# Where the modulation of a second block is summed: from the expert stages to the projections and the gated layers, in 1024-column steps

## The reference

```python
mod = (jax.nn.silu(c) @ w_ada[l] + b_ada[l])[:, None, :]          # c: [1, 1024], w_ada: [1024, 9 * 1024]
sh1, sc1, gt1, sh2, sc2, gt2, sh3, sc3, gt3 = jnp.split(mod, 9, axis=-1)
n = modulate(rmsnorm(h, g_ffn1[l]), sh1, sc1)                     # n * (1 + scale) + shift
h = h + 0.5 * gt1 * swiglu(n, w1_gate[l], w1_up[l], w1_down[l])
n = modulate(rmsnorm(h, g_mix[l]), sh2, sc2)
h = h + gt2 * hybrid_mixer(n, w_in[l], w_pool[l], pool_scale[l], w_out[l])
n = modulate(rmsnorm(h, g_ffn2[l]), sh3, sc3)
h = h + 0.5 * gt3 * swiglu(n, w2_gate[l], w2_up[l], w2_down[l])
```

## Time and profile before

| what | value |
| --- | --- |
| median of 3 runs | 1484.13 us (1484.05 to 1486.57) |
| the profiled execution: its time, its span | 1485.72 us, 1483.6 us |
| PE busy | 1410.2 us, 95% |
| VectorE busy | 971.9 us, 66% |
| ScalarE busy | 697.3 us, 47% |
| moved by the DMA engines | 266.48 MB, mean 180 GB/s |

### The profile page before, as it was taken

One profiled execution on the slowest core, in us unless ns is written; L12 is line 12 of the kernel. 1 busy time (PEld: TensorE's weight loads), 2 busy tenths in 40 slices (PEclk: granted clock), 3 DMA queues, 4 the chain that ended last, 5 costly groups with the idle time before them and its releaser, 6 DMA issues.

```text
span 1483.6 us, 16900 instructions
## 1 busy us (share of the span) xinstructions
PE 1410.2 (95%) x6579; PEld 1149.5 (77%) x6579; DVE 971.9 (66%) x1449; ACT 697.3 (47%) x1014; POOL 18.6 (1%) x41
## 2 busy tenths in 40 slices
PE   7979999999999998999999999989999899899997
PEld 5856677888888877777887887778888787778885
DVE  4577647677577777667767678745777557544444
ACT  6464536434343567453343443644434455443442
POOL 0000000000000000000000000000000000000000
PEclk9987999999999998999999999999999999999999
DMA  8440015466555542044665666534656452455530
GB/s 330 171 146 1 1 64 220 158 266 256 234 227 230 227 168 89 29 152 179 266 247 230 267 255 266 194 119 174 251 227 232 189 196 86 131 188 181 195 114 29
DMA packets 37902, 266.48 MB, mean 180 GB/s; under 512 B 4525, under 2 KB 5040, under 8 KB 6080
## 3 DMA queue, kind: packets, MB, share of 16 engines
q1 hardware_dynamic: 36720, 262.65, 46.8%
q0 software_dynamic: 960, 2.52, 0.6%
q10 hardware_dynamic: 144, 0.24, 0.0%
HBM read 264.34 MB, written 1.05 MB: 179 GB/s over the span
## 4 chain that ended last, share of the span: by engine, by line
PE 88%; DVE 8%; ACT 2%; issue 1%; DMA 0%; POOL 0%; DVEq 0%; ACTq 0%; POOLq 0%
PE ps L373 25%; PE ps L375 24%; PE ps L374 24%; DVE wl L1138 2%; PE ps L391 2%; PE ps L552 2%; PE ps L489 1%; PE ps L649 1%; DVE AR L1301 1%; DVE KL L1206 1%; PE ps L467 1%; PE ps L477 1%; ACT XN L835 1%; PE ps L470 1%; PE ps L454 1%
## 5 line engine op out<-in xcount | busy, mean ns | idle before, releaser
L1138 DVE TENSOR_TENSOR wl<-ring,wh 128x2048 fp32r<-128x2048 f32 x208 | 471.7, 2288 | 162.6 <-ACT wh L823 162.3
L373 PE MATMUL ps<-wh,XH 128*128 128x512 f32 x1216 | 481.8, 396 | 6.6 <-DVE wl L1138 5.1
L375 PE MATMUL ps<-wh,XL 128*128 128x512 f32 x1216 | 475.4, 391 | 0.0
L374 PE MATMUL ps<-wl,XH 128*128 128x512 f32 x1216 | 474.8, 390 | 0.0
L823 ACT ACTIVATE wh<-ring 128x2048 fp32r<-128x2048 f32 x208 | 393.4, 1912 | 144.7 <-PE ps L375 144.2
L373 PEld LDWEIGHTS ps<-wh,XH 128*128 128x128 f32 x1216 | 229.3, 189 | 55.3 <-issue 6.0
L375 PEld LDWEIGHTS ps<-wh,XL 128*128 128x128 f32 x1216 | 229.1, 188 | 48.7
L374 PEld LDWEIGHTS ps<-wl,XH 128*128 128x128 f32 x1216 | 229.6, 189 | 46.0
L373 PE MATMUL ps<-wh,HT 128*128 128x512 f32 x448 | 176.9, 395 | 6.0 <-DVE HT L1393 4.5
L375 PE MATMUL ps<-wh,HT 128*128 128x512 f32 x448 | 174.6, 390 | 0.0
L374 PE MATMUL ps<-wl,HT 128*128 128x512 f32 x448 | 174.4, 389 | 0.0
(11 more groups left out here) (235 smaller groups left out, 1150.3 us busy)
## 6 DMA issues: line engine op xcount, KB each, us to landing
ring<-stream_dram SPq DMA_DIRECT2D x248, 1024.0 KB, 7.0
H<-x_dram SPq DMA_DIRECT2D x2, 512.0 KB, 4.7
out_dram<-XN SPq DMA_DIRECT2D x2, 512.0 KB, 2.7
XN<-ag_dram POOLq DMA_DIRECT2D x1, 768.0 KB, 4.6
AR<-pT_dram POOLq DMA_DIRECT2D x2, 256.0 KB, 3.0
AR<-g_final_dram POOLq DMA_DIRECT2D x1, 512.0 KB, 4.1
ring<-stream_dram SPq DMA_DIRECT2D x2, 144.0 KB, 5.4
VBK<-w_pool_dram POOLq DMA_DIRECT2D x1, 256.0 KB, 3.3
```

What stands on the lines that cost most here:

```text
L373: e.matmul(o, ah, bh, start=start, stop=False)
L374: e.matmul(o, ah, bl, start=False, stop=False)
L375: return e.matmul(o, al, bh, start=False, stop=stop)
L1138: e.tensor_tensor(wl[:, k % WBUF, :], ring[:, n % RING, :], h.bitcast(F32), ALU.subtract).then_inc(up("wlo", ("wlo", k)))
```

## The change

The nine parts are made elsewhere: part 0 in nsa (4 quarters in 4 steps, at `kv0`, `kv1`, `kv2`, `q0`), part 1 in moba (4 quarters in 3 steps, at `skv`, `bq0`, `bq1`: 1, 1, 2), parts 2 to 6 in `ffn1` (20 quarters in 10 pairs, two a pair), part 7 in the mixer (3 steps, 1, 1, 2), part 8 in `ffn2` (4 quarters in 6 pairs). The expert stages have none. A quarter is now two of the eight rows of each partition over all 1024 columns of the part: one chunk, two instructions of 1024 columns. The biases of shifts and scales come as 48 columns of the constants and are added after the turn (one more tensor_tensor, 128 x 8); the bias row is left for the gates. `silu(c)` is made in nsa. Sums: part 0 after `q1`, part 1 after `bq1`, part 7 after `z3`, part 8 in `ffn2`; in `ffn1` parts 2 to 5 at pairs 2, 4, 6, 8 and part 6 at 11, that is behind the last `down`.

```diff
-ADA = {0: (0, 1, 3), 1: (2, 5, 4, 6), 2: (7, 8)}
+ADA = {"nsa": (0,), "moba": (1,), "ffn1": (2, 3, 4, 5, 6), "mixer": (7,), "ffn2": (8,)}
+ADA_STEPS = {"nsa": 4, "moba": 3, "ffn1": 10, "mixer": 3, "ffn2": 6}
...
-        return [("ada", v[:, :, 256 * q:256 * q + 256]) for q in ada_quarters(l, j)]
+        return [("ada", v[:, 2 * (q % 4):2 * (q % 4) + 2, 1024 * (q // 4):1024 * (q // 4) + 1024]) for q in ada_quarters(stage, j)]
...
-    for c in (1024, 1536, 2048):
-        plan += w_cols(w_in, c, 512)
-    plan += compress("a_ck_w1") + w_cols(w_in, 0, 512) + compress("a_cv_w1") + w_cols(w_in, 512, 512)
+    for i, c in enumerate((1024, 1536, 2048)):
+        plan += w_cols(w_in, c, 512) + ada("nsa", i)
+    plan += compress("a_ck_w1") + w_cols(w_in, 0, 512) + ada("nsa", 3) + compress("a_cv_w1") + w_cols(w_in, 512, 512)
...
+            plan += w_cols(w["w_kv_shared"], 0, 512) + ada("moba", 0)
+            for i, c in enumerate((0, 512)):
+                plan += w_cols(w["b_w_q"][0], c, 512) + ada("moba", i + 1)
...
-        plan += pairs_plan(16, gu, down, lambda j: ada(l, j))
+        plan += pairs_plan(16, gu, down, lambda j: [])
...
+        for stage in ("ffn1", "ffn2"):
+            for j in range(12):
+                ada_due[stage, j] = [q // 4 for i in ((j - 1,) if j < 10 else () if j == 10 else (9, 10)) for q in ada_quarters(stage, i) if q % 4 == 3]
...
                 project("bq1", "mix1", lambda t: [("bqsq", 1, t)])
+                ada_sum(1)
                 turn_heads(("bt", 0), QN[:, :, 0:512], 8, [("bn", 0)])
...
+                    take(len(ada_quarters("nsa", c)))
...
+            def ada_turned(part):
+                c = 2 * (part // 3) + part % 3
+                dst = MT[:, 8 * c:8 * c + 8]
+                for hf in range(2):
+                    e.wait_ge(*at("adasum", part, hf))
+                    e.tensor_reduce(dst[:, 4 * hf:4 * hf + 4], ps("ada", part, hf)[:, :].rearrange("p (a n) -> p a n", a=4), AX,
+                                    ALU.add).then_inc(up("dve", ("turnsum", part, hf)))
+                e.wait_ge(*at("turnsum", part, 1))
+                e.tensor_tensor(dst, dst, col("ab", 8 * c, 8), ALU.add).then_inc(up("dve", ("mod", part)))
...
+            def ada_take(q):
+                take()
+                part, f, a = q // 4, q % 4, ACC[q // 4]
...
+                for t in range(2):
+                    c, v = SC8[:, 2 * f + t:2 * f + t + 1], r[:, 1024 * t:1024 * t + 1024]
+                    if f + t == 0:
+                        ins = e.tensor_scalar(a, v, c, None, ALU.mult)
+                    else:
+                        e.wait_ge(*at("adaq", 8 * part + 2 * f + t - 1))
+                        ins = e.scalar_tensor_tensor(out=a, in0=v, scalar=c, in1=a, op0=ALU.mult, op1=ALU.add)
...
                     e.tensor_reduce(ss2[:, t, 0:4], heads(SQ[:, t, 0:256]), AX, ALU.add).then_inc(up("dve", ("skvss", t)))
+                ada_step("moba", 0)
                 feature_major("mix1", free=[("pj", "skv", 1)])
...
                         e.tensor_reduce(qss[:, t, 8 * c:8 * c + 8], heads(SQ[:, t, :]), AX, ALU.add).then_inc(up("dve", ("bqss", c, t)))
+                    ada_step("moba", c + 1)
                     if c == 0:
                         low("skt", 4, lambda j: KS[1][:, j, :], lambda j: KS[0][:, j, :], col("ks"), True)
                         q_norm("bn", "broot", 0)
+                ada_turned(1)
                 low(("bt", 0), 8, q_of, q_of, S[:, 8:9])
...
-                take(6)
+                for i in range(3):
+                    take(2)
+                    ada_step("mixer", i)
                 low("zk", 8, lambda j: KS[1][:, j, :], lambda j: KS[0][:, j, :], None, True)
                 take(2)
+                ada_turned(7)
                 low("zq", 8, lambda j: q_of(j, 4), lambda j: q_of(j, 4), None)
```

More of the change, by code:

```diff
@@ L162, in down @@
             return rows(w[f"w{i}_down_2"][0][256 * j:256 * j + 256])
-        return pairs_plan(11, gu, down, lambda j: ada(2, j) if i == 1 else [])
+        return pairs_plan(11, gu, down, lambda j: ada(f"ffn{i}", j))
     plan += ffn(1)
-    for c in (1024, 512, 0, 1536):
-        plan += w_cols(w["w_in_2"][0], c, 512)
+    for i, c in enumerate((1024, 512, 0, 1536)):
+        plan += w_cols(w["w_in_2"][0], c, 512) + (ada("mixer", i) if i < 3 else [])
     for c in (0, 512):
@@ L510, in attention, with ada_sum, ada_sums @@
                         values(i - 3)
[L512 to L524, removed]
+            def ada_sum(part):
+                e.wait_ge(*at("ada", part))
+                if part % 3 == 2:
+                    for hf in range(2):
+                        b = bank("ada", part, hf, by=[("gate", part, hf)])
+                        e.matmul(b[:, :], ones[:, :], ACC[part][:, half(hf)], start=True, stop=True).then_inc(up("full", ("adasum", part, hf)))
+                else:
+                    for hf in range(2):
+                        b = bank("ada", part, hf, by=[("turnsum", part, hf)])
+                        for u in range(4):
+                            ins = e.transpose(b[:, tok(u)], ACC[part][:, 4 * hf + u:1024:8], ID)
+                        ins.then_inc(up("full", ("adasum", part, hf)))
+            def ada_sums(stage, j):
+                for part in ada_due[stage, j]:
+                    ada_sum(part)
             def gated(name, n, view, rows=None, l=None):
@@ L809, in one @@
             def one(self):
+                while self.next not in split_no:
+                    self.next += 1
                 self.next += 1
@@ L901, in attention, with ada_sums @@
                             e.activation(XH[:, jo + j, :], ps("o", name, j)[:, 0:256], ACT.Copy, scale=1.0).then_inc(up("xraw", ("xh", name, j)))
-            def ada_sums(l, j):
-                for part, _ in ada_due[l, j]:
+            def ada_sums(stage, j):
+                for part in ada_due[stage, j]:
                     if part % 3 == 2:
@@ new lines, in ada_turned @@
+            def ada_turned(part):
+                c = 2 * (part // 3) + part % 3
+                dst = MT[:, 8 * c:8 * c + 8]
+                for hf in range(2):
+                    e.wait_ge(*at("adasum", part, hf))
[3 more added lines that the diff above has]
+                e.tensor_tensor(dst, dst, col("ab", 8 * c, 8), ALU.add).then_inc(up("dve", ("mod", part)))
+                if part % 3 == 1:
+                    e.wait_ge(*at("mod", part))
+                    e.scalar_tensor_tensor(out=dst, in0=dst, scalar=1.0, in1=col(f"g{part // 3 + 1}", 0, 8), op0=ALU.add,
+                                           op1=ALU.mult).then_inc(up("dve", ("mod", part)))
@@ L1309, in first_of, with ada_takes, ada_step @@
+            def ada_takes(stage, j, last):
+                qs = ada_quarters(stage, j)
+                for q in qs[-1:] if last else qs[:-1]:
+                    ada_take(q)
+            def ada_step(stage, j):
+                for q in ada_quarters(stage, j):
+                    ada_take(q)
             def first_of(l, x, mx, n, names, ready):
```

150 lines of the change are left out of this document (64 added, 86 removed).

## The result

The changed kernel takes 1523.49 us (median of 4 runs, 1516.98 to 1529.76) against 1485.35 us before (4 runs beside it, 1484.05 to 1486.73): ratio 1.0256, 95% interval 1.0209 to 1.0304. The forecast was 1525.5 us with a range of 1499 to 1537. The profiled execution is the shortest of the four, 1516.98 us with a span of 1515.1.

The account below looks back on a forecast made before the run. Matmul-bound almost everywhere; VectorE work matters only where its in-order queue holds up TensorE. -17.3 + 6.9 + 18.75 + 11.3 + 13.9 + 1.35 + 6.8 = +41.7 us, giving 1525.5 us; range 1499 to 1537.

Parts of the forecast that it names:

- expert stages: Both expert stages: seven sums and the stalls of pairs with two quarters go away, -4.05 and -13.2, together -17.3 us.
- ada_turned(0): nsa, just before the attention: two reduces of 512 columns and an add where VectorE is late, +1.6 us.
- moba, up to `low`: moba's projections: later splits, quarters and the wait for part 1's sum delay the feature-major split and first `low`, +18.75 us.
- mixer, up to `low("zq")`: Mixer: last projection 3.1 us late; quarters, splits and part 7's turn stand before `low("zq")`, on which the scores wait, +11.3 us.
- The moved splits: Projections: inserted chunks count in the look-ahead, so second-half splits are issued behind ScalarE's copies; `blocks` 6.3, moba's feature-major split 6.0 us late.
- Rival B: Whole kernel: only the quarters themselves are paid, no moved splits and no clock, 1500 us; chance 0.14.
- rival A: Whole kernel: the steps are really hidden in VectorE's idle stretches, so the kernel gets faster, 1471 us; chance 0.06.
- pair 0 term: ffn1, pair 0: the split of `down(0)` falls behind `turn_hidden(0)`, +3.4 us, plus 1.7 us of clock.
- The tail: End of ffn1: part 6's reduces wait for transposes after the last `down`, then all of `sum_up` follows, 6.25 against 1.45, +4.8 us.
- The ten pairs: ffn1, two quarters a pair: two more sums 2.7 us, late splits in six pairs 2.5 us, pair 9 0.5 us.
- Rival C: ffn1: transfers of the added chunks land 1 us late each pair, ScalarE waiting for `ring`, 1535 us; chance 0.10.
- The clock: TensorE idles ahead of `q0`, `bq0`, `down(0)` and the mixer's attention lower the granted clock: 4 x 1.7 = 6.8 us, bounds 0 and 10.

Follow-up runs that it names:

- skip_ahead: The changed kernel, but modulation chunks don't count in the look-ahead of the splits; 1521.75 us, ratio 1.0242.
- moba_back: The changed kernel with part 1 taken out of moba and made in the first expert stage; 1502.68 us, ratio 1.0114.
- late6: The changed kernel with part 6's sum made in the mixer, just ahead of part 7's, not behind ffn1's last down; 1518.71 us, ratio 1.0217.
- even: The change's new form, but one quarter a pair in expert and feed-forward stages, none in projections; 1473.02 us, ratio 0.9916 to the kernel before.
- even_rot: The kernel with one quarter a pair everywhere, with two PSUM banks passed over ahead of the turns of nsa's first queries; 1475.16 us, ratio 0.9927.
- nsa_back: The changed kernel with part 0 taken out of nsa and made in the first expert stage; 1525.07 us, ratio 1.0278; profiled twice.
- wide_only: The kernel before with its placement kept and only the quarters' form changed to two 1024-column instructions, biases as columns; 1476.79 us, ratio 0.9937.
- mixer_back: The changed kernel with part 7 taken out of the mixer and made in the first expert stage; 1523.09 us, ratio 1.0241; profiled twice.
- both_back: The changed kernel with parts 1 and 7 both made in the first expert stage; 1502.16 us, ratio 1.0114.

## Why the prediction was right

Step by step, in the first profile of the changed kernel. The total there is +31.5 us of span.

| step | forecast | measured |
| --- | --- | --- |
| expert stages | -17.3 | -16.0 |
| nsa, up to the first `low` | +5.3 and 1.7 of clock | +6.1 |
| nsa's attention | +1.6 (`ada_turned(0)`) | -2.7 (bank) |
| moba, up to `low` | +18.75 and 1.7 | +20.8 |
| mixer, up to `low("zq")` | +11.3 | +11.1 to 11.5 |
| ffn1 | +13.9 and 1.7 | +16.7 |
| ffn2 | +1.35 | +1.75 |
| attentions of moba and mixer | +1.7 | -5.6 and -1.0 |

Three numbers of the forecast are slightly off without bearing on it. 1527.4 less 1.6 is 1525.8, not 1525.5. VectorE's time falls by 47 us (134.7 to 87.5 in its groups), not by over 50. And a sum was charged 1.35 us of whatever kind, the mean of the two in `ffn1`. By the table a shift or scale costs 0.92 and a gate 1.76, which is why three shifts and scales less give 3.4 us (2.8 for the sums, the rest for the old form) where 4.05 were forecast, and why `ffn2` with its gate pays 1.75 and not 1.35.

**The moved splits** were the largest term and came as worked out. In nsa `blocks` is 6.2 us late (forecast 6.3). In moba the feature-major split starts at 553.62 against 548.14, 5.5 us late (forecast 6.0; half of the difference is the first step, 0.75 instead of 1.0). TensorE waits 3.27 us for the last mixer projection (3.1), but only 4.1 us in three waits ahead of its attention, not 7, as its transposes and the pooling fill the rest; the start of `low("zq")`, which sets the end, is as forecast. skip_ahead shows the mechanism by itself: 10.0 of moba's 20.8 us and 7.0 of the mixer's 11.1 go away when the splits are issued early, and what is left is the quarters' own time. Rival B, which paid for the quarters alone, falls with it, and rival A with moba_back, where one part's four quarters cost 20.8 us in moba and 0.9 in the expert stage.

**ffn1.** The pair 0 term was 3.4 and 1.7; the second hidden turn is 4.95 us late (1021.08 - 1013.63 less the 2.50 by which the stage started late). The tail was 4.8 and is 4.4 (the last add starts 5.1 us behind the last `down` matmul, 0.8 before), and late6 gives 3.1 of it back. The ten pairs cost 7.4 instead of 5.7: pairs of 17.5 and 18.6 us follow each other (without and with a sum), where 16.8 is the length with one quarter and no sum (even).

The late pairs are the ones that were forecast. In the timeline TensorE idles ahead of the gate/up products in six pairs, released by the split: 0.36 us in four and 0.31 and 0.53 in the two whose reduces come first, 2.27 in all (2.5 in the forecast). In the pairs that sum a gate it doesn't idle, though ScalarE's two copies stand before the next high part and VectorE's split waits 1.28 us for it: the first product at 1050.38 follows the `down` products at once. The rows are VectorE's and TensorE's of a gate's pair, then TensorE's of a late pair.

```profile
1047.53 4.49 DVE L1146 TENSOR_TENSOR wl<-ring,wh 128x2048 fp32r<-128x2048 f32 x2 [1.28 <-ACT wh L826]
...
1050.38 0.39 PE L368 MATMUL ps<-wh,XH 128*128 128x512 f32 x1
```

```profile
1031.69 0.47 PE L368 MATMUL ps<-wh,XH 128*128 128x512 f32 x1 [0.36 <-DVE wl L1146]
```

The term that was too small is the loss in a late pair. Between the starts of the two matmuls around such a wait pass 0.69 to 0.91 us (0.75 in the pair shown), against 0.23 between others: 3.2 us in the six pairs, and 0.65 at the last hidden turn, for which 0.5 was taken. That makes 3.9 us where the forecast had 3.0, beside the 2.7 for the two more sums; the last 0.8 us of the 7.4 is not attributed.

Rival C does not hold in the changed kernel. Between 1010 and 1170 us the DMA engines moved 292 GB/s at a share of 0.76, and ScalarE never waited for the ring. A wait of its kind appears in skip_ahead, where splits are asked for earlier: ScalarE waits for the ring there. That the ring's depth is the bound follows from the order of the chunks and was not tested by a deeper ring.

**A miss inside the sum**: `ada_turned(0)` was charged 1.6 us. It cost nothing, and its two banks took away a wait of 10.66 us that the kernel before has ahead of its scores, 2.7 us of it net. The forecast read that wait nowhere. even_rot shows the cause, and nsa_back the way back: without the two banks the wait is 10.66 us again and the attention 120.41.

**The clock** was charged as four stalls of 1.7 us, 6.8. At the three places where a stage starts cold, 0.8, 2.1 and 1.55 us are over the queue's own cost, near it. These are remainders; the granted clock itself is 0.50 there from 65.4 to 68.3, 554.6 to 559.8 and 1007.4 to 1010.4 us, where the kernel before has 1.00 in the same products. The fourth stall was put at the wrong place: the clock is 1.00 all through the mixer's attention, and 0.64 from 1237.9 to 1242.4, behind the wait of 3.27 us ahead of the last mixer projection, which was charged none. But the attentions moved as much and in both directions, which the forecast had no term for. The profiled execution recovered 6.7 us there and stands at +31.5; the median of the runs stands at +38.1. The total of 41.7 came out near the median partly because this term happened to fall so: outside the attentions of moba and mixer the change costs 38.1 us (1393.7 - 1355.6), the forecast had 40.0 for that.

What sets the clock in moba's attention is open. Its length was 55.5 and 55.8 in before and wide_only, 49.9 and 52.9 in two executions of the changed kernel, 65.0 twice in mixer_back, 65.1 and 55.4 in nsa_back. Neither the stall in front (3.0 us in both_back, 12.7 in mixer_back and in the changed kernel) nor the way the attention is computed decides it. Executions of one kernel differ, and a kernel can also favour one length.

## What to carry to other kernels

Price a piece of work by the queue it is put in, not by its duration: with one quarter a pair the four quarters of a part cost nothing beyond the part's sum (0.92 us for a shift or scale, 1.76 for a gate); a part costs 3.9 us in `ffn1` with two a pair (five parts: 183.89 less 167.16 - 2.69), 11 in the mixer and 21 in moba, where VectorE's in-order work is what TensorE waits for. When chunks are put into a list that a look-ahead counts, look at every later take that now issues its splits later, and if you correct it, at the depth of the ring. And compare kernels stage by stage between the same rows before believing a median: here some 9 us gained outside the attentions (mixer_back) were swallowed whole by the clock in one of them.

## What was not expected of the hardware

After a stretch in which TensorE was partly idle, the granted clock in moba's attention was 0.50 for 30 us and more while TensorE's row is busy for 10.00 of 10.00 us (three such rows of mixer_back, and in both_back the rows from 578 to 628; a matmul's end is modelled in the profile, so busy is not proof of a full engine). The Trainium skill (TensorE: Matmul & The Clock Gate, "What's actually happening") has the clock released by activity. If the busy time of these rows is such activity, by that page they would have run at 2.4 GHz after their beginning; the trace disagrees. The same instructions ran at 1.00 in the changed kernel (606 to 626), and the difference is 18.3 us between both_back and the changed kernel on the same attention.

Eight instructions of 256 columns took 3.8 us a quarter and two of 1024 columns take 2.57. That is (3.8 - 2.57) / 6 = 0.2 us for each instruction saved, an estimate from these rows.
